# Grouped heads of an attention layer: score, max and shift products of two steps interleaved in halves and quarters of the array

## What is computed

```python
xn = rms_norm(h, norm_in[l])
proj = jnp.einsum('bsd,dn->bsn', xn, w_in[l])
a_q, a_k, a_v, a_g, b_cq, b_ckv, b_kr, b_g = jnp.split(proj, _SPLITS, axis=-1)
# grouped heads: 8 query heads, 2 key/value heads, width 64, RMS norm and 2-D rotary
y_a = blocked_attention(q, k, v)
# latent heads: 4 heads, query/key width 96, value width 128, from normalised latents
y_b = blocked_attention(qb, kb, vb)
y = jnp.concatenate([y_a * jax.nn.silu(a_g), y_b * jax.nn.silu(b_g)], axis=-1)
h = h + jnp.einsum('bsm,md->bsd', y, w_out[l])

def one_block(qblk):           # inside blocked_attention
    s = jnp.einsum('bkgqd,bksd->bkgqs', qblk, k).astype(jnp.float32) * scale
    p = jax.nn.softmax(s, axis=-1).astype(v.dtype)
    return jnp.einsum('bkgqs,bksd->bkgqd', p, v)
```

## Time and profile before

| | us |
|---|---|
| median of 3 runs | 1577.34 (1576.66 to 1577.96) |
| profiled execution | 1578.2 |
| its span, first to last instruction | 1576.4 |
| TensorE busy in the span | 1533.0 (97%) |
| VectorE / ScalarE / GpSimd busy | 1306.5 / 1233.3 / 590.6 |

### The profile page before, as it was taken

One profiled execution on the slowest core, in us unless ns is written; L12 is line 12 of the kernel. 1 busy time (PEld: TensorE's weight loads), 2 busy tenths in 40 slices (PEclk: granted clock), 3 DMA queues, 4 the chain that ended last, 5 costly groups with the idle time before them and its releaser, 6 DMA issues.

```text
span 1576.4 us, 37757 instructions
## 1 busy us (share of the span) xinstructions
PE 1533.0 (97%) x13326; PEld 887.9 (56%) x13326; DVE 1306.5 (83%) x1952; ACT 1233.3 (78%) x1668; POOL 590.6 (37%) x506
## 2 busy tenths in 40 slices
PE   6999999999997999999999999999999999999999
PEld 3555555555553565566566566656656655654444
DVE  6886676776787988998998998899899899987764
ACT  8777677667656888888888888888888888867663
POOL 0100000000002665666666666566666666640000
PEclk9999999999999999999999999999999999999999
DMA  9444453444323543244234324324423432636663
GB/s 332 117 131 81 109 120 69 111 107 71 84 63 100 119 101 77 68 107 95 61 79 97 79 63 108 70 66 106 97 61 78 97 79 63 147 98 214 203 198 106
DMA packets 251044, 166.70 MB, mean 106 GB/s; under 512 B 65424, under 2 KB 230800, under 8 KB 250992
## 3 DMA queue, kind: packets, MB, share of 16 engines
q1 hardware_dynamic: 227632, 151.48, 38.0%
q10 hardware_dynamic: 22464, 13.63, 3.1%
q0 software_dynamic: 896, 0.93, 0.8%
HBM read 119.16 MB, written 40.93 MB: 102 GB/s over the span
## 4 chain that ended last, share of the span: by engine, by line
PE 53%; DVE 10%; issue 4%; ACT 1%; DVEq 0%; ACTq 0%
PE p_acc L2082 5%; DVE hand_part L1892 5%; PE p_st L2045 5%; PE p_st L2046 5%; PE p_acc L2086 4%; PE hand_mx L2013 4%; PE p_acc L2088 4%; PE p_acc L2087 3%; PE p_st L2049 3%; PE p_st L2048 3%; PE p_st L1502 3%; PE p_st L1505 3%; PE p_st L1503 3%; PE hand_mx L2015 3%; DVE p_pl L1920 3%
## 5 line engine op out<-in xcount | busy, mean ns | idle before, releaser
L1791 POOL TENSOR_TENSOR p_pl<-p_p,p_ph 128x512 f16<-128x512 f32 x384 | 508.6, 1330 | 287.2 <-ACT p_ph L1830 225.9
L1892 DVE TENSOR_REDUCE hand_part<-hand_mx 128x2 f32<-128x1024 f32 x373 | 454.8, 1219 | 68.9 <-PE hand_mx L2013 50.8
L1821 ACT ACTIVATE p_p<-p_st 128x1024 f32<-128x1024 f32 x384 | 390.9, 1018 | 96.6 <-PE p_st L2053 52.5
L1197 PE MATMUL p_ring<-p_w_hi,p_xT 128*128 128x512 f16 (+3 forms) x1536 | 391.0, 340 | 8.4 <-DVE p_w_lo L905 5.9
L1830 ACT ACTIVATE p_ph<-p_p 128x1024 f16<-128x1024 f32 x334 | 353.1, 1057 | 18.3
L1920 DVE TENSOR_TENSOR p_pl<-p_p,p_ph 128x512 f16<-128x512 f32 x384 | 331.7, 865 | 0.6
L1197 PE MATMUL p_ring<-p_w_lo,p_xT 128*128 128x512 f16 (+3 forms) x768 | 260.8, 340 | 0.0
L1197 PEld LDWEIGHTS p_ring<-p_w_hi,p_xT 128*128 128x128 f16 x1536 | 151.2, 98 | 129.3 <-issue 7.2
L2082 PE MATMUL p_acc<-p_vas,p_ph 128*128 128x129 f16 x2048 | 207.9, 221 | 0.1
L2082 PEld LDWEIGHTS p_acc<-p_vas,p_ph 128*128 128x128 f16 x2048 | 180.7, 97 | 36.5 <-issue 17.6
L2083 PE MATMUL p_acc<-p_vas,p_pl 128*128 128x65 f16 x2048 | 201.0, 193 | 0.0
(11 more groups left out here) (195 smaller groups left out, 2364.2 us busy)
## 6 DMA issues: line engine op xcount, KB each, us to landing
p_vbs<-scratch_vb SPq DMA_DIRECT2D x16, 1028.0 KB, 6.4
p_xin<-in_x SPq DMA_DIRECT2D x16, 512.0 KB, 7.9
p_xcol<-in_x_cols SPq DMA_DIRECT2D x16, 512.0 KB, 6.7
scratch_g<-p_g SPq DMA_DIRECT2D x16, 512.0 KB, 3.4
p_kb<-scratch_kb SPq DMA_DIRECT2D x32, 256.0 KB, 5.4
p_vas<-in_x SPq DMA_DIRECT2D x16, 512.0 KB, 3.9
out<-p_ph SPq DMA_DIRECT2D x15, 512.0 KB, 2.9
out_gt<-scratch_g ACTq DMA_DIRECT2D x13, 512.0 KB, 3.5
```

Source lines behind the costliest of these rows:

```text
L1197: last = pe.matmul(ring_t[:, 0:w], a, b, start=(k == 0 and m == 0), stop=(k == len(steps) - 1 and m == len(terms) - 1))
L1791: pool.tensor_tensor(pl[:, s % NP, 1, :], p32[:, s % N32, QB:], ph[:, s % NP, 1, :], ALU.subtract).then_inc(s_lop, 1)
L1821: act.activation(p32[:, s % N32, :], st[:, s % 2, :, :].rearrange("p a b -> p (a b)"), ACT.Exp, scale=scale).then_inc(s_exp, 1)
L1892: dve.tensor_reduce(part[:, e // MPAIRS % 3, 2 * c:2 * c + 2], mx[:, :, :], AX, ALU.max).then_inc(s_red, 1)
```

## The change

Six of the 16 grouped steps of an iteration (`PAIRED`: 0 and 1, 2 and 3, 14 and 15) are taken two at a time by a new function `grouped_pair`, in all iterations but the first, and in the last one only 0 to 3. There the second product over 128 rows is split. The low queries times the high keys become products of 64 rows, in the upper half (`low_top`, from a new copy `qa_low`) or the lower half (`low_bottom`) of the array. The maxima are taken off by products of two rows (`shifted`: `ones` against `shift`) that lie in a quarter of the array, with copies of the two rows at rows 0, 32, 64 and 96. For these, `max_rows` issues eight more DMAs for each grouped unit, counted on the same semaphore, and `rows_done` waits for 160 where it waited for 32. The second block of the first step of a pair gets its low product below, the first one above; the first block of the second step gets its low product at the end of the first step, after a wait for the exponential (`s_exp`, n). The wait for `s_red` stands before the low products. SyncE also loads `qa_low`, and GpSimd fills `ones` at the start.

```diff
+    PAIRED = (0, 1, 2, 3, 14, 15)
+        qa_low = sb("qa_low", [64, GA, QB], F16)
+        shift = sb("shift", [P, GA, QB], F16)
+        ones = sb("ones", [P, P], F16)
...
-            eng.wait_ge(s_mr[pos], (i + 1) * (32 if UNITS[pos][1] == "a" else 64))
+            if pos == 0:
+                eng.wait_ge(s_mr[0], i * 160 + 32)
+            else:
+                eng.wait_ge(s_mr[pos], (i + 1) * (160 if UNITS[pos][1] == "a" else 64))
...
+                if kind == "a":
+                    for r0 in (0, 32, 64, 96):
+                        for r in range(2):
+                            sp.dma_start(shift[r0 + r:r0 + r + 1, g, :], mpair[:, pos, r, :]).then_inc(s_mr[pos], 16)
...
+            def grouped_pair(i, s):
...
+                if s % STEPS == 0:
+                    rows_done(pe, i, pos)
...
+                def direct(b, new):
+
+                    return pe.matmul(st[:, s % 2, b, :], ka_hl[g][:, block(s, b)], qa_hh[g][:, :], start=new, stop=False)
+
+                def low_top(step, b, new):
+
+                    return pe.matmul(st[:, step % 2, b, :], ka_hl[g][0:64, block(step, b)], qa_low[:, g, :], start=new, stop=False)
+
+                def low_bottom(b):
+
+                    return pe.matmul(st[:, s % 2, b, :], ka_up[g][64:128, block(s, b)], qa_ml[g][64:128, :], start=False, stop=False)
...
+                def shifted(b, r0):
+
+                    return pe.matmul(st[:, s % 2, b, :], ones[r0:r0 + 2, :], shift[r0:r0 + 2, g, :], start=False, stop=True)
+
+                if first_step:
+                    pe.wait_ge(s_exp, n - 1)
+                    for b in range(2):
+                        direct(b, True)
+                    pe.wait_ge(s_red, n + LEAD)
+                    if c == 0:
+                        loaded(i + u // 3, u % 3)
+                    low_top(s, 0, False)
+                    low_bottom(1)
+                    max_top(0)
+                    for b in range(2):
+                        end = shifted(b, 64 + 32 * b)
+                    end.then_inc(s_st, 1)
+                    pe.wait_ge(s_exp, n)
+                    max_bottom(1).then_inc(s_mx, 1)
+                    low_top(s + 1, 0, True)
+                else:
+                    direct(0, False)
+                    direct(1, True)
+                    pe.wait_ge(s_red, n + LEAD)
+                    if c == 0:
+                        loaded(i + u // 3, u % 3)
+                    max_top(0)
+                    low_bottom(1)
+                    max_bottom(1).then_inc(s_mx, 1)
+                    for b in range(2):
+                        end = shifted(b, 32 * b)
+                    end.then_inc(s_st, 1)
...
-                    scores(i, s, first)
-                    if not (last and s + LEAD >= HALF):
-                        max_pair(i, s + LEAD, False)
+                    if s in PAIRED and not first and not (last and s + LEAD >= HALF):
+                        grouped_pair(i, s)
+                    else:
+                        scores(i, s, first)
+                        if not (last and s + LEAD >= HALF):
+                            max_pair(i, s + LEAD, False)
```

More of the change, by code:

```diff
@@ L1561, in phase2 @@
         s_q = [sem(f"q_loaded{p}") for p in range(3)]
+        s_ql = [sem(f"q_low_loaded{g}") for g in range(GA)]
         s_kb = sem("kb_loaded")
@@ L1642, in load_q, with load_q_low @@
                         sp.dma_start(dst.rearrange("r (two t) -> r two t", two=2), src[r0:r1]).then_inc(s_q[pos], 16)
+            def load_q_low(i, g):
+                src = QA[1].rearrange("(g h) (q two) r t -> g (h q) r two t", g=GA, two=2)[g, i]
+                sp.dma_start(qa_low[:, g, :].rearrange("r (two t) -> r two t", two=2), src).then_inc(s_ql[g], 16)
             def load_kb(h):
@@ L1712, in place_piece @@
                 sp.dma_start(o.w[n // KT][:, :, n % KT, :], o.w_new[:, :, :]).then_inc(o.s_win, 16)
+            load_q_low(0, 1)
             for i in range(N):
@@ L1719, in _ @@
                     load_q(i + 1, 0)
+                    load_q_low(i + 1, 0)
                 if i == 0:
@@ L1743, in _ @@
                     load_q(i + 1, 1)
+                    load_q_low(i + 1, 1)
                 if i == 0:
@@ L1797, in body @@
                         unit_of(i, COPY_AT[s], unit, first)
+            pool.memset(ones[:, :], ONE).then_inc(s_const, 1)
+            pool.wait_ge(s_const, 1)
             pool.memset(kb_3[32:34, :], ONE).then_inc(s_const, 1)
             pool.memset(kb_3[96:98, :], ONE).then_inc(s_const, 1)
-            pool.wait_ge(s_const, 2)
+            pool.wait_ge(s_const, 3)
             loop(pool, body)
@@ L2016, in max_pair, with max_top, max_bottom @@
                 mm.then_inc(s_mx, 1)
+            def grouped_pair(i, s):
+                pos = s // STEPS
+                g = UNITS[pos][0]
+                n = i * HALF + s
+                first_step = s % 2 == 0
+                if s % STEPS == 0:
+                    rows_done(pe, i, pos)
+                if first_step and s % STEPS in (0, 6):
+                    pe.wait_ge(s_const, 3)
+                    if pos == 0:
+                        pe.wait_ge(s_ql[0], i * 16)
+                    else:
+                        pe.wait_ge(s_ql[1], i * 16 + 16)
+                u = (s + LEAD) // MPAIRS
+                gm, c = UNITS[u % 3][0], (s + LEAD) % MPAIRS
+                queries = slice(c // 2, QB, QT)
+                block = lambda step, b: slice((step % STEPS * 2 + b) * P, (step % STEPS * 2 + b + 1) * P)
+                def direct(b, new):
[4 more added lines that the diff above has]
+                    return pe.matmul(st[:, s % 2, b, :], ka_up[g][64:128, block(s, b)], qa_ml[g][64:128, :], start=False, stop=False)
+                def max_top(x):
+                    k0 = (c % 2 * 2 + x) * QB
+                    return pe.matmul(mx[:, x, :], qa_hh[gm][0:64, queries], ka_hl[gm][0:64, k0:k0 + QB], start=True, stop=True)
+                def max_bottom(x):
+                    k0 = (c % 2 * 2 + x) * QB
+                    return pe.matmul(mx[:, x, :], qa_hh[gm][64:128, queries], ka_up[gm][64:128, k0:k0 + QB], start=True, stop=True)
+                def shifted(b, r0):
[28 more added lines that the diff above has]
+                    end.then_inc(s_st, 1)
@@ L2034, in scores @@
                     if kind == "b":
-                        pe.wait_ge(s_const, 2)
+                        pe.wait_ge(s_const, 3)
                         pe.wait_ge(s_kb, i * 96 + 96)
```

## The result

| | before | after |
|---|---|---|
| median of 4 runs, us | 1577.0 (1572.9 to 1578.0) | 1712.8 (1708.8 to 1719.0) |
| profiled execution, us | 1578.2 | 1712.6 |
| mean granted TensorE clock | 0.998 | 0.966 |

The ratio is 1.087 (95% interval 1.085 to 1.090): 136 us slower. The forecast was slower, by 66 us, with 1656 us as the upper end of the range.

A forecast was written before the change was run, and what follows sets the result against it. PE bounds the kernel from step 18 round to 13, DVE in steps 14 to 17. Waits 20.0 + 19.5, pairs 20.7 + 6.2 = 66.4 us on the 1577.3 us median: 1643 us, range 1606 to 1656.

The forecast's parts named there:

- the clock: PE's granted clock in phase 2: taken as full, with no term for a fall behind the new waits.
- the row copies: Ten copies make PE wait 1.57 us before step 8 and 1.33 before step 0: 19.5 and 20.0 us in all.
- The array: Paired steps' split products on PE: from 0.17 us less to 0.54 us more per pair; upper end taken.
- The serial case: Paired steps: each height change is paid, nothing overlaps; 0.54 us more per pair on PE, 1643 us total, chance 0.55.
- only from half to half: PE's weight loads: claimed to be pulled ahead only between half-height products; a height change costs 0.10 us.
- side by side: Rival for paired steps: quarter products run beside halves, 0.17 us less per pair on PE; 1616 us, chance 0.27.
- partly: Rival for paired steps: quarter load waits only for its own rows, not pulled ahead; 9 us more, 1625 us, chance 0.12.
- The moved wait for the reduction: PE waits for the previous reduction before the low products: 0.15 us per early pair, covered at step 0.
- the 0.35 us that PE was to regain in step 9 or 10: After step 8's wait PE regains 0.35 us lost to DVE, leaving 1.22 of 1.57 us, x 16.

The follow-up runs named there:

- run 1: Changed kernel with no steps taken as pairs; only the ten row copies and the waits for them stay: 1657.6 us, ratio 1.053.
- run 2: Changed kernel with six row copies in place of ten, so the rows are in time; all pairs of steps stay: 1606.9 us, ratio 1.020.
- run 3: Changed kernel with nine extra full-height products of 512 columns in front of each wait for rows, results overwritten: 1667.3 us, ratio 1.059.
- Run 4: Changed kernel with six row copies, 34-row half-height products (zero-padded) taking off the maxima, and another product order within pairs: 1587.3 us, ratio 1.008.
- run 6: Changed kernel with eight row copies (rows 32, 64 and 96) in place of ten, shortening the waits: 1626.4 us, ratio 1.032.

## Why the prediction was wrong

The step that failed is the clock, which the sum put at nothing; the row copies were too small by a third. The 136 us fall into three parts: waits for rows 58 us (the iterations of run 1 at full clock), pairs on the array 32 us (run 2), clock 45 us (run 3 against the changed kernel). They add up to 135. The first two are tested by run 3, which has both at full clock: +93 us for 58 + 32 = 90. The clock's part is a difference and less sharp: 43 us when each is set against its own runs of before, and 50 us from the changed kernel's own trace (from step 0 at 557.5 to step 0 at 1474.5 us are 14 iterations, 917 us, where 14 x 61.9 = 867 would be full clock).

**The array: right.** The serial case was chosen for the bounds, and its numbers held: two-row pair 0.31 us behind a half product, the next half product 0.32 us behind it; steps 0 to 3 +1.35 us for a forecast +1.38, steps 14 to 17 +0.45 for +0.44. Run 4 agrees from the other side: without quarters, and in another order, 20 of 32 us are gone. One reading beside it was loose: loads are hidden within any one height, not "only from half to half", as the full products 0.215 us apart show. The rival "side by side" and the one called "partly" fall with the trace.

**The moved wait for the reduction: right.** 0.15 us, covered at step 0 by the wait for rows, seen by itself in run 2 (2.59 for 2.43 us). In the changed kernel's step 1 the low product comes 0.68 us after the first score (691.97 to 692.65), 0.14 us later than in step 0 (689.53 to 690.07).

**The row copies: right in mechanism, too small in size.** The term was 39.5 us and measured 58. There are three parts. One is the issue: 0.64 us for each of the eight, where I took half of 1.18 us from a group of two. The row with four together (2.47 us, 0.62 each) was nearer to ten in a row; I had kept it for the range. A second is that the sum let PE start with the landing: its first score came 0.1 to 0.3 us after it. The third is the 0.35 us that PE was to regain in step 9 or 10. I read it from one iteration (6). Half of the iterations of before have only 0.03 us to regain there: the timeline of iterations 1 to 5 gives 56.07 us, that of 6 gives 56.39. With 7.9 us for the tenth copy and the mean of both I would have had 16 x (2.1 - 0.2) + 15 x 1.96 = 60 us. One small delay that the forecast had put at nothing came too: in the first iteration PE waits 1.42 us at step 16 (536.52 us) for the copies of the latent unit's rows, which before it did not.

**The clock: missing.** This is the step that failed. The text took the clock as "full", which it was, and asked only what a wait of 1.3 to 1.6 us adds, not whether it might halve the clock of what follows: the sum had no term for it, and 43 to 50 us were measured. A row of before, not among those that I had read for the stage, gives a warning; it is the passage from phase 1 to phase 2, where PE waits twice:

```profile
480.00:500.00 20.00, 15.66 (x59) 5.63 (x59) 12.81 (x24) 10.08 (x22) 1.57 (x1) 0.83 0.22 70
```

The two waits, and finer windows behind them:

```profile
482.06 0.62 PE L223 MATMUL hand_mx<-early 64*128 64x512 f16 x2 [3.31 <-DMA early<-hand_kept]
498.47 0.41 PE L2013 MATMUL hand_mx<-early 64*128 64x512 f16 x2 [2.15 <-PEq L235]
...
481.00:487.00 6.00, 4.94 (x13) 1.79 (x14) 3.68 (x5) 5.84 (x14) 0.00 (x0) 0.50 0.40 148
...
498.40:508.00 9.60, 7.98 (x54) 3.53 (x54) 8.57 (x10) 9.36 (x11) 6.90 (x5) 1.00 0.78 208
```

The clock is down around the wait of 3.31 us and full behind the one of 2.15 us. So before showed that a wait can halve the clock, but only for a wait twice as long as those that I priced; that shorter ones do it too came from the changed kernel. Waits of 1.7 to 2.8 us let the clock fall in a part of the cases (17 of 31 in the changed kernel, 11 of 31 in run 1), waits of 0.5 to 1.0 us (and one of 1.7) in none (run 6), and a wait in which PE computes in none (run 3). What decides which of the waits do it, these runs leave open. What the forecast could not have had from any row is that the pairs with quarter products right behind the wait keep the clock down for some 10 us: the waits alone (with their short falls of the clock) took 83 us and the pairs alone 32, together 115, but the kernel with both took 136.

## What to carry to other kernels

Treat a product's height as a state of the whole array: count the changes of height in a sequence, 0.10 us each and nothing beside them, before counting what could run side by side; a product padded with zero rows to its neighbours' height, in a changed order, was cheaper than a small one. When an engine waits for a series of small DMAs, price the last of the series with the issue gap of a long series, and set it against the distance that the first had. Where a new wait stops PE for a us or two, ask for the granted clock behind every such stop, and cost the work behind it at both levels.

## What was not expected of the hardware

- A stop of PE of about 2 us was enough for the clock to fall to its lower level in some of the cases, for 3.4 us; with quarter-height products behind it the fall lasted 10.2 us, with half-height products in another order 3.4 us. Why is open.
- Nine superfluous products in the wait made the kernel 45 us faster.
- Two small DMAs less per grouped unit (ten to eight) were worth 86 us, as the wait fell from 2.0 to about 0.7 us and with it the clock loss.
